# Two products run beside a delta-rule chain: column block by column block, or weight unit by weight unit over four PSUM banks

## The reference, cut to what matters

```
proj = xn @ w_in
# branch A: gated delta rule, 4 heads of 128; chunks of 64 tokens
sol = triangular_solve(eye + m, rhs)          # per chunk and head; u, w = split(sol)
def step(state, inp):                         # a scan over the chunks
    v_new = u_c - w_c @ state
    o = qd_c @ state + qk_c @ v_new
    state = state * ge_c + kd_c.T @ v_new
# branch B: stick-breaking attention, 8 heads of 64
q_b = rms(proj_q) * gain; k_b = rms(proj_k) * gain
...
x + merged @ w_out
```

## Time and profile before

| | |
|---|---|
| three runs | 1715.75, 1718.77, 1725.13 us (median 1718.77) |
| the profiled execution: its time | 1715.52 us |
| its span, first to last instruction | 1713.7 us |
| mean granted clock of TensorE | 0.937 of full |
| busy share of the span | PE 88%, PEld 66%, DVE 55%, ACT 42%, POOL 4% |

### The profile page before, as it was taken

The page is one execution under the profiler, slowest core; times in us unless marked ns, Lnnn a source line. Parts: engine busy times, 40 slices in busy tenths (PEclk is TensorE's granted clock), DMA queues, the critical chain, the costliest instruction groups (busy, mean ns, idle before and its releaser), DMA issues.

```text
span 1713.7 us, 17589 instructions
## 1 busy us (share of the span) xinstructions
PE 1506.8 (88%) x7159; PEld 1132.7 (66%) x7159; DVE 947.0 (55%) x1301; ACT 717.2 (42%) x1045; POOL 70.0 (4%) x72
## 2 busy tenths in 40 slices
PE   5999989899999647999999946997888999999999
PEld 4888866676678534555555525766767876678887
DVE  3444247754856356888888845856654444322344
ACT  4333234553552205666666623435221125643221
POOL 1000000000000002111110010000000000000000
PEclk9999999999999867999999977998998978999999
DMA  6522321131233408999999962202000012002241
GB/s 201 175 85 87 99 74 50 49 99 50 74 125 110 163 23 271 331 338 337 326 336 335 330 217 99 74 25 74 1 26 25 1 50 98 1 1 81 92 147 50
DMA packets 78683, 219.81 MB, mean 128 GB/s; under 512 B 8915, under 2 KB 10053, under 8 KB 74502
## 3 DMA queue, kind: packets, MB, share of 16 engines
q1 hardware_dynamic: 70534, 191.63, 33.1%
q0 software_dynamic: 5504, 18.62, 3.3%
q10 hardware_dynamic: 2560, 8.39, 1.3%
HBM read 197.91 MB, written 20.71 MB: 128 GB/s over the span
## 4 chain that ended last, share of the span: by engine, by line
PE 61%; DVE 26%; ACT 10%; issue 2%; DMA 1%; SPq 1%; POOL 0%; DVEq 0%; POOLq 0%; ACTq 0%
PE PS L506 15%; PE PS L508 14%; PE PS L507 14%; DVE wlo L1149 6%; DVE htlo L1149 5%; PE PS L925 4%; ACT whi L1947 3%; DVE ylo L1149 2%; PE PS L503 2%; PE PS L1074 2%; ACT yhi L1947 2%; ACT hthi L1947 2%; PE PS L1065 2%; ACT work L1947 1%; DVE work L1558 1%
## 5 line engine op out<-in xcount | busy, mean ns | idle before, releaser
L1149 DVE TENSOR_TENSOR wlo<-raw,whi 128x2048 fp32r<-128x2048 f32 x74 | 169.5, 2291 | 329.9 <-ACT whi L1947 329.9
L1947 ACT ACTIVATE whi<-raw 128x2048 fp32r<-128x2048 f32 x74 | 141.5, 1912 | 311.3 <-PE PS L508 301.0
L506 PE MATMUL PS<-whi,hthi 128*128 128x512 f32 x480 | 198.7, 414 | 9.9 <-ACT work L1947 6.4
L506 PE MATMUL PS<-hthi,whi 128*128 128x512 f32 x480 | 197.5, 411 | 11.0 <-DVE work L1269 6.4
L503 PE MATMUL PS<-consts,work 128*128 128x128 f32 (+1 forms) x652 | 98.2, 293 | 108.7 <-DVE work L1175 53.3
L508 PE MATMUL PS<-whi,htlo 128*128 128x512 f32 x480 | 189.3, 394 | 0.0
L507 PE MATMUL PS<-wlo,hthi 128*128 128x512 f32 x480 | 188.9, 394 | 0.0
L508 PE MATMUL PS<-hthi,wlo 128*128 128x512 f32 x480 | 188.8, 393 | 0.0
L507 PE MATMUL PS<-htlo,whi 128*128 128x512 f32 x480 | 188.7, 393 | 0.0
L503 PEld LDWEIGHTS PS<-consts,work 128*128 128x128 f32 (+1 forms) x652 | 83.1, 179 | 137.9 <-DVE work L1175 54.4
L1947 ACT ACTIVATE work<-PS 128x512 f32<-128x512 f32 (+3 forms) x204 | 103.1, 529 | 95.4 <-PE PS L989 51.3
(11 more groups left out here) (321 smaller groups left out, 2651.8 us busy)
## 6 DMA issues: line engine op xcount, KB each, us to landing
raw<-in_w_in SPq DMA_DIRECT2D x44, 1024.0 KB, 5.0
raw<-in_w SPq DMA_DIRECT2D x80, 512.0 KB, 5.6
scratch<-in_w SPq DMA_DIRECT2D x48, 512.0 KB, 6.3
raw<-in_w SPq DMA_DIRECT2D x19, 1024.0 KB, 8.6
scratch<-in_w SPq DMA_DIRECT2D x13, 1024.0 KB, 9.0
raw<-in_w_gate SPq DMA_DIRECT2D x8, 1024.0 KB, 5.1
raw<-in_w_out SPq DMA_DIRECT2D x8, 1024.0 KB, 6.4
y_scratch<-work ACTq DMA_DIRECT2D x32, 256.0 KB, 7.0
```

The costliest lines, as they stand in the source:

```text
L506: e.matmul(o, lh, rh, start=start, stop=False)
L1149: tt(lo, raw_place(j), as_f32(hi), SUB).then_inc(*ve.mark("lo", j))
L1947: return e.activation(o, i, f, bias=bias, scale=scale)
```

## The change

TensorE runs "qb" and "kb" with `part` instead of `natural_in_steps`: first the sixteen triples of a product's first unit, over four column blocks that fill four banks at the same time, then the sixteen of the second unit. The pauses go: "kb" follows "qb" at once. ScalarE and VectorE read the banks at the steps at which they are now filled (19, 23, 27, 31 of each product's 32 steps). The four splits stand at steps 18, 34, 50 and 66 (`SPLITS`; `GATED` is 64). "qb" is scaled as soon as its mean is there, "kb" four steps later.

```
@@ constants
-    PAUSE = 5
@@ tensor
-        def natural_in_steps(name, b, ready):
-            j0, n = unit[name, b]
-            parts = [tuple(halves(j0 + kh)) for kh in range(n)]
-            kt = n * HB
-            for c in range(HB):
-                cols = slice(c * P, c * P + P)
-                ps = fresh(name, b, c)
-                for kk in range(kt):
-                    wh, wl = parts[kk // HB]
-                    on.wait_ge(*ve["lo", j0 + kk // HB])
-                    on.wait_ge(*ready)
-                    m = passes(ps, hthi[:, kk, cols], htlo[:, kk, cols], wh[:, kk % HB, :], wl[:, kk % HB, :],
-                               kk == 0, kk == kt - 1)
-                    if kk < kt - 1:
-                        yield
-                m.then_inc(*pe.mark(name, b, c))
-                bank.filled((name, b, c))
-                if c == HB - 1:
-                    for kh in range(n):
-                        pe.also("unit", j0 + kh)
-                yield
 
         def beside_steps():
             for name in ("qb", "kb"):
-                yield from natural_in_steps(name, 0, h_ready)
-                for _ in range(2 * PAUSE):
-                    yield
+                for kh in range(2):
+                    yield from part(name, 0, kh, False, hthi, htlo, h_ready)
@@ vector
         def beside_steps():
-            for name in ("qb", "kb"):
+            def steps(first, n):
+                for step in range(first, first + n):
+                    if step in SPLITS:
+                        split()
+                    yield
+
+            def normed(name):
+                r = inverse_root(name, 32)
+                settle()
+                d = beside_nat[name].rearrange("p (g d) -> p g d", d=SBD)
+                on.wait_ge(*ac["out", name, 0, HB - 1])
+                tt(d, d, bc(r, [P, 32, SBD]), MUL).then_inc(*ve.mark(name, 0, "normed"))
+
+            for n, name in enumerate(("qb", "kb")):
+                at = n * KD * HB
+                yield from steps(at, HB * HB)
                 for c in range(HB):
-                    for _ in range(KD):
-                        yield
+                    yield from steps(at + HB * HB + c * HB, HB)
                     on.wait_ge(*ac["squares", name, c])
                     red(stat[name][0][:, c * SBH:(c + 1) * SBH], beside_sq.rearrange("p (g d) -> p g d", d=SBD),
                         ADD).then_inc(*ve.mark("sums", name, c))
                 settle()
                 mean_square(name, 32, SBD)
-                split()
-                yield
-                r = inverse_root(name, 32)
-                settle()
-                d = beside_nat[name].rearrange("p (g d) -> p g d", d=SBD)
-                on.wait_ge(*ac["out", name, 0, HB - 1])
-                tt(d, d, bc(r, [P, 32, SBD]), MUL).then_inc(*ve.mark(name, 0, "normed"))
-                for _ in range(PAUSE - 1):
-                    yield
-                split()
-                for _ in range(PAUSE):
-                    yield
+                if n == 0:
+                    normed(name)
+            yield from steps(GATED, HB)
+            normed(name)
@@ scalar
         def beside_steps():
             before = None
-            for name in ("qb", "kb"):
+
+            def steps(first, n):
+                ...
+
+            for n, name in enumerate(("qb", "kb")):
                 dst = tiles(beside_nat[name])
+                at = n * KD * HB
+                yield from steps(at, HB * HB)
                 for c in range(HB):
-                    for _ in range(KD - 1):
-                        yield
+                    yield from steps(at + HB * HB + c * HB, HB - 1)
                     on.wait_ge(*pe[name, 0, c])
                     ...
                     yield
-                split()
                 root(name, 32)
-                for _ in range(PAUSE):
-                    yield
-                split()
-                for _ in range(PAUSE):
-                    yield
+            yield from steps(GATED, HB)
```

## The result

The changed kernel takes 1730.15 us (median of nine runs, 1726.74 to 1731.79) where the kernel before, run beside it on the same chip, takes 1717.69 (nine runs, 1714.85 to 1725.22). The ratio is 1.0054, 95% interval 1.0032 to 1.0076: about 9 us slower (the two medians alone are 12.5 apart). Its profiled execution took 1730.56 us, span 1728.6, at a mean granted clock of 0.931 (0.937 before).

What follows compares the result with a forecast made beforehand. TensorE bounds in the inversion levels, chains of DVE and ACT answers in openings and bare states. Terms -3.0 + 3.1 + 0.5 = +0.6 us on a median of 1718.77 gave 1719.4, range 1708 to 1729.

Steps and rivals of the forecast that it cites:

- The forecast of no change: Whole kernel: +0.6 us, a median of 1719.4; a result of same had a chance of 0.67.
- the side with a chance of 0.13: Whole kernel: the changed kernel comes out measurably slower than before.
- the line of 0.5%: Whole kernel: about 8.6 us, taken as what a measurement can tell from no change.
- all three terms: Pause -3.0 us, vb0's split in round 25 +3.1, bare end +0.5.
- the clock falls and stays: Rival: pause and bare end run at half clock for most of their length, +12.0 us, 1731; chance 0.12.
- Step 1: Pause, rounds 16 to 20: added triples, kb0's split gone, kv with qS at full clock, -3.0 us (-4.5 to +4.4).
- the row it was set against: Tile 3's opening in the profile before: gaps of 1.6 and 2.0 us cost only one short clock dip.
- Step 2: Round 25, tile 3's opening: vb0's split delays DVE's chain and PE, +3.1 us (+1.7 to +4.7).
- Step 3: Rounds 32 to 41 without triples: the chain and vb1's split bound, +0.5 us (-10.4 to +4.5).
- Step 4: kb0's split in round 9, loads, vb1's split before the chains' end, four held banks: no cost (banks' bound +3).
- Its signs of being wrong: Clock far from about 0.9 in the pause and 0.6 at the end, or PE waiting on ACT for a bank.

Runs made afterwards that it cites:

- fill_after: The changed kernel with matmuls nobody reads added in the waits from the openings to tile 3's last states: 0.9893 of the kernel before, median 1699.95 us.
- fill_before: The kernel before with matmuls nobody reads added in the openings, tile 2's two long waits and tile 3's states: 0.9914 of the kernel before, median 1706.36 us.
- splits_late: The changed kernel with its three later splits moved out of openings and bare states (steps 42, 58 and behind the chains): 0.9965 of the kernel before.
- fill_open: splits_late plus five and seven matmuls nobody reads before the two waits in all four openings: 0.9887 of the kernel before.
- units_only: The kernel before with only the new unit-by-unit order over four banks; pauses and split steps kept, "qb" scaled ahead of kb0's split: 1.0030 of the kernel before.
- before_again: The kernel before, unchanged, run for a second profile: 1720.17 us.
- after_again: The changed kernel, unchanged, repeated in a second series: 1.0032 of the kernel before, median 1727.78 us.

## Why the prediction was wrong where it was

The forecast of no change, 1719.4, did not come true. The median, 1730.15, lies just above the range of 1708 to 1729 (by the ratio, 1.0054 x 1718.77 = 1728.1, just inside). By the first comparison the side with a chance of 0.13 came; by the repeat, 1.0032, the loss is under the line of 0.5%. Where the range held, it did so because it was wide: all three terms missed to the same side, by 6.0, 0.9 and 2.2 us. What happened is the rival that the text called "the clock falls and stays", in a milder form: +8.3 in place of +12.0.

**Step 1, the pause, is the step that failed.** It said "-3.0 us", and it was +3.0. Its order of work was right up to the decay matmul. The decay matmul began 14.0 us after round 16 (said: 14.5), the wait for L1742 is gone, and that start is 1.6 us sooner than before. What failed is "it takes 4.42 instead of 7.40". From the decay matmul to `kv` it was 13.32 us instead of the 10.9 worked out, and `kv` with `qS` took 7.80, since the clock fell twice, to 0.66 at 1290 and to 0.55 and 0.50 from 1300. The prediction had reasoned that triples in the pause would hold the clock. But they run ahead of the waits, not in them: no triple stands between `kk` and `qk` and the transposes that wait for DVE's answer to these. The waits of 1.51 and 2.00 us were the same in both kernels, and so was the fall behind them. With the waits filled the same two stretches are 10.64 (1277.13 to 1287.77 in fill_after) and 4.4, as the step had them.

The gain itself was nearly all clock. Of the -3.0, the 4.42 in place of 7.40 was -3.0, and the earlier start of `kv` and the added triple cancelled. It set the changed order at full clock against the order before at half clock. At full clock in both, rounds 16 to 20 take 28.6 us in the order before (fill_before) and 29.9 in the changed one (fill_after): moving the triples there wins nothing.

What the prediction cited from the Trainium skill ("TensorE: Matmul & The Clock Gate", A second HAM failure mode: psum-queue depth-cycling), that short idle gaps between matmul groups make the clock swing, was the better guide than the row it was set against. This trace agrees: the clock fell behind the opening of tile 2 in every kernel whose gaps were left (0.50 in splits_late), and stayed at 1.00 in fill_open, where they were filled.

**Step 2, vb0's split, was right in mechanism and a little small.** "+3.1" was +4.0. The wait came at 4.59 (said: 4.7), with `wlo` in front of DVE's L1726. The other 1.0 us is the low clock behind the longer wait (the transposes, a triple at 0.63 a matmul), which the step had in its upper bound of +4.7. With the clock held the split costs 1.9 (22-33: 52.36 in fill_after, 50.51 in fill_open).

**Step 3, the bare end, was right up to 13.5 us and then wrong.** "+0.5" was +3.3 up to `kv` of round 38, less 0.6 behind it: +2.7. `qS` ended at 6.3, `wlo` at 11.1, and `kv` began at 13.52 (said: 13.6). Then "full clock again after them" did not come: `nw`, `u` and `wS` ran at half clock too (the groups of eight at 1394.91, 1396.77 and 1398.48 start 1.86 and 1.71 apart instead of 0.81), and `kv` came at 29.3 instead of 27.3, nearer to the 30.0 of the bound of +4.5. The sum had a slip as well: 23.9 and the 3.0 us of `kv` and `qS` at half clock are 26.9, not 27.3, so the step was +0.1 by its own terms.

**Step 4 was right.** No wait for kb0's split in round 9 shows in the changed kernel, and none for a bank there or in units_only. The gap for want of PSUM that the Trainium skill names ("Perfetto Trace Analysis", Identifying Performance Opportunities), weighed there, did not appear.

**Its signs of being wrong.** The wait at L1755 (4.59), the wait behind vb1's `wlo` (2.75) and the clock at the end (0.56, said about 0.6) came as said. The clock of the pause did not: 0.79 where about 0.9 was named, and round 21 came 3.0 us later, not sooner.

**What the prediction missed altogether** is kb1's split, which stands in the pause in both kernels (round 18, then 17), in front of tile 2's opening, so that the working carried it along and never asked what it cost. It was the largest thing to be had in the pause: 5.6 us in splits_late, of which 3.1 are DVE's time (22.20 in fill_after, 19.14 in fill_open); the rest goes with the clock.

**The balance.** In both filled kernels the clock is 1.00 in each of the table's first four columns, so these can be parted. Over them the kernel before loses 8.5 us against its own filled version (125.25, 116.79) and the changed one 17.6 (133.24, 115.66). With the clock held the two orders are 1.1 us apart, less than two profiles of one kernel differ by; the clock takes 9.1 more from the changed one: +8.0. Each is one profile, good to some 1.5 us, and the fillers were not the same, so this is a division in size, not to the decimal. In the last column the two kernels are alike (33.72, 33.47), and fill_before, not held there, gives no comparison. That the lost time is clock is shown by these profiles; that the timed ratio of fill_after to fill_before is below one is not.

**Left open:** why the runs of one kernel lie up to 19 us apart, why units_only is slower in time than its trace explains, and how much of the changed kernel's loss between series (1.0054 and 1.0032) is the phase described below.

## What to carry to other kernels

Work of VectorE and ScalarE that only has to be done some time, as a weight's split, belongs where TensorE is full; in front of a chain of answers it costs its length and then the clock of everything behind it. When a move is priced, each new or remaining wait of TensorE can have a second price, the matmuls behind it at half clock. In these runs spare matmuls that ran ahead of the work whose answer is awaited did not save that price; those that ran between that work and the answer did. A kernel before that runs a stretch at half clock also makes every move into that stretch look better than it is, so both sides should be priced at the same clock. If TensorE's waits can't be shortened, fill them with matmuls that nobody reads, and stop where the wait, not the clock, sets the time.

## What the hardware showed that was not expected

**Two short waits cost more than themselves.** Waits of 1.51 and 2.00 us, with 0.66 us of transposes between, were followed in the changed kernel by half clock while PE was busy 9.35 of 10 us: 1300 to 1310 at 0.55 and 0.50. `kv` with `qS` alone lost 3.4 us (7.80 against 4.42). It was the same in splits_late, where these two were the only waits of the pause: 7.79 us at 0.50.

**Useless work made the kernel 0.8% faster** (splits_late 0.9965, fill_open 0.9887), and the unchanged kernel before by 0.9% (fill_before).

**The openings of tiles 0 and 1 take a different time from one execution to the next.** From the first transposes to `kv` of round 15, with the same order of work, it was 71.24 (before), 70.11 (before_again), 71.32 (after_again), and 73.79 in the changed kernel's first profile; with the openings filled it was 68.52 (fill_open) and 68.50 (fill_after). So up to 4 us of the difference between two single profiles can come from this alone. The first transposes themselves stood anywhere from 1190.84 to 1195.83 in these four profiles.
